# Loading the input X in two halves of 64 partitions from two DMA queues

## The reference

```
x = layer_norm(x, ln_in_g, ln_in_b)
c_act = silu(c)
ada = c_act @ w_ada + b_ada            # shift, scale and gate vectors, 9 of width 1024
h = x * (1 + scale) + shift            # the first of the three modulations
x = layer_norm(ALPHA * x + 0.5 * gate * swiglu(h, ffn1_w_in, ffn1_w_out), ...)
```

## Time and profile before

| | |
|---|---|
| median of 3 runs | 1103.38 us (1103.23 to 1103.72) |
| the profiled execution, its time | 1103.3 us |
| its span, from the first to the last instruction | 1101.5 us |
| granted clock of the matrix engine | 1.00 |
| PE busy | 1094.1 us (99% of the span) |
| DVE, ACT, POOL busy | 520.8, 415.3, 510.8 us |
| data moved | 142.11 MB, mean 129 GB/s |

### The profile page before, as it was taken

The page is one execution under the profiler, slowest core; times in us unless marked ns, Lnnn a source line. Parts: engine busy times, 40 slices in busy tenths (PEclk is TensorE's granted clock), DMA queues, the critical chain, the costliest instruction groups (busy, mean ns, idle before and its releaser), DMA issues.

```text
span 1101.5 us, 15344 instructions
## 1 busy us (share of the span) xinstructions
PE 1094.1 (99%) x5568; PEld 894.5 (81%) x5568; DVE 520.8 (47%) x934; ACT 415.3 (38%) x671; POOL 510.8 (46%) x274
## 2 busy tenths in 40 slices
PE   9999999999999999999999999999999999999998
PEld 6788888888888997875578888898888888888887
DVE  6767755441121269368747677684222223211105
ACT  5552332223222284278623233357222222232223
POOL 1035554444454464357824454646444444445452
PEclk9999999999999999999999999999999999999999
DMA  9555555322333272210136654414433332233322
GB/s 368 208 188 202 179 194 172 105 96 86 92 102 105 74 256 100 87 58 1 49 125 209 218 167 150 150 43 138 150 115 114 114 114 95 90 93 102 105 70 77
DMA packets 53747, 142.11 MB, mean 129 GB/s; under 512 B 5824, under 2 KB 14016, under 8 KB 52416
## 3 DMA queue, kind: packets, MB, share of 16 engines
q1 hardware_dynamic: 52976, 136.40, 37.6%
q10 hardware_dynamic: 720, 5.03, 1.2%
HBM read 139.31 MB, written 2.10 MB: 128 GB/s over the span
## 4 chain that ended last, share of the span: by engine, by line
PE 96%; DMA 1%; DVE 1%; SPq 1%; ACT 0%; issue 0%; POOL 0%; ACTq 0%; DVEq 0%
PE psum L711 30%; PE psum L713 29%; PE psum L712 29%; PE psum L1124 2%; PE psum L1203 2%; PE psum L1175 2%; DMA ada_first<-in_ada 1%; PE psum L1059 1%; PE psum L741 1%; PE psum L1189 0%; PE psum L1095 0%; SPq L518 0%; PE psum L849 0%; ACT tokens L1511 0%; PE psum L1041 0%
## 5 line engine op out<-in xcount | busy, mean ns | idle before, releaser
L600 POOL TENSOR_TENSOR w_lo<-raw,w_hi 128x1024 fp32r<-128x1024 f32 x171 | 422.4, 2475 | 505.3 <-ACT w_hi L1315 505.3
L711 PE MATMUL psum<-h_hi,w_hi 128*128 128x512 f32 (+1 forms) x1006 | 381.3, 379 | 0.2 <-POOL h_lo L654 0.2
L713 PE MATMUL psum<-h_hi,w_lo 128*128 128x512 f32 (+1 forms) x1006 | 378.0, 376 | 0.0
L712 PE MATMUL psum<-h_lo,w_hi 128*128 128x512 f32 (+1 forms) x1006 | 377.9, 376 | 0.0
L1315 ACT ACTIVATE w_hi<-raw 128x1024 fp32r<-128x1024 f32 x178 | 186.4, 1052 | 144.6 <-PE psum L713 94.6
L711 PEld LDWEIGHTS psum<-h_hi,w_hi 128*128 128x128 f32 x1006 | 189.2, 188 | 39.2 <-issue 4.5
L713 PEld LDWEIGHTS psum<-h_hi,w_lo 128*128 128x128 f32 x1006 | 189.3, 188 | 34.7
L712 PEld LDWEIGHTS psum<-h_lo,w_hi 128*128 128x128 f32 x1006 | 189.3, 188 | 33.4
L2054 DVE SCALAR_TENSOR_TENSOR acc<-ada_raw,cact,acc 128x512 f32<-128x512 f32 x98 | 138.5, 1448 | 16.7 <-DMA ada_raw<-in_ada_w 16.6
L711 PE MATMUL psum<-act_hi,w_hi 128*128 128x512 f32 (+1 forms) x396 | 145.3, 367 | 0.0
L713 PE MATMUL psum<-act_hi,w_lo 128*128 128x512 f32 (+1 forms) x396 | 144.7, 365 | 0.0
(11 more groups left out here) (300 smaller groups left out, 1013.1 us busy)
## 6 DMA issues: line engine op xcount, KB each, us to landing
raw<-in_ffn_in SPq DMA_DIRECT2D x81, 512.0 KB, 3.2
ada_raw<-in_ada_w SPq DMA_DIRECT2D x112, 256.0 KB, 3.5
raw<-in_ffn_out SPq DMA_DIRECT2D x32, 448.0 KB, 3.3
raw<-in_mix_w SPq DMA_DIRECT2D x27, 512.0 KB, 3.3
ada_first<-in_ada SPq DMA_DIRECT2D x8, 1024.0 KB, 7.8
raw<-in_ffn_out SPq DMA_DIRECT2D x16, 512.0 KB, 3.5
raw<-in_branch_w SPq DMA_DIRECT2D x8, 512.0 KB, 3.9
raw<-in_mixout_w SPq DMA_DIRECT2D x8, 512.0 KB, 3.4
```

Of the source, the lines that this page charges most:

```text
L600: gp.tensor_tensor(w_lo[:, slot, :], raw[:, slot % 2, :], w_hi[:, slot, :].bitcast(F32), ALU.subtract).then_inc(split_done, 1)
L711: pe.matmul(o_, w[0][:, wslot, ws], xh, start=first, stop=False)
L712: pe.matmul(o_, w[0][:, wslot, ws], xl, start=False, stop=False)
L713: return pe.matmul(o_, w[1][:, wslot, ws], xh, start=False, stop=last)
```

## The change

Each of the five pieces of X is issued as two DMAs of 64 partitions: partitions 0 to 63 by SP as before, partitions 64 to 127 by ACT, before ACT's first table load. Both raise the same semaphore of the piece by 16, so everyone who waits for a piece waits for 32 in place of 16. No other transfer, and no computation, is changed.

```
-                sp.dma_start(X[:, a:z, :], xT[:, a:z, :]).then_inc(x_landed[i], 16)
+                sp.dma_start(X[0:64, a:z, :], xT[0:64, a:z, :]).then_inc(x_landed[i], 16)
...
-                    pe.wait_ge(x_landed[i], 16)
+                    pe.wait_ge(x_landed[i], 32)
...
+            for i, (a, z) in enumerate(X_LOADS):
+                act.dma_start(X[64:P, a:z, :], xT[64:P, a:z, :]).then_inc(x_landed[i], 16)
             act.preload_act_table(ACT.Tanh)
             for m in SQ_ACT:
-                act.wait_ge(x_landed[X_LOAD_OF[m]], 16)
+                act.wait_ge(x_landed[X_LOAD_OF[m]], 32)
                 act.activation(hbuf[:, m, :], X[:, m, :], ACT.Square).then_inc(x_squared_act, 1)
-            act.wait_ge(x_landed[X_LOAD_OF[KT - 1]], 16)
+            act.wait_ge(x_landed[X_LOAD_OF[KT - 1]], 32)
...
-                dve.wait_ge(x_landed[X_LOAD_OF[m]], 16)
+                dve.wait_ge(x_landed[X_LOAD_OF[m]], 32)
```

## The result

| | before | after |
|---|---|---|
| median | 1103.35 us (17 runs, 1103.18 to 1103.88) | 1105.61 us (17 runs, 1105.31 to 1106.1) |
| ratio | | 1.0021, 95% interval 1.0014 to 1.0027 |
| span of the profiled execution | 1101.5 us | 1103.9 us |

The change costs 2.26 us. The forecast was 1103.3 with a range up to 1104.5, so the time lies outside of it. It is about the size that the prediction called the edge of what can be told (2.2 us); with 17 runs each the interval is clear of 1, so the loss is real, though small.

A forecast was written before the change was run, and what follows sets the result against it. PE's gapless matmuls were taken to bound the kernel, so only the head, where loads stand in one line, counts. Terms -0.20 + 0.15 = -0.05 us on 1103.3 made 1103.25, with 0.08 for the median 1103.3; range 1102.6 to 1104.5.

The forecast's parts named there:

- What bounds the kernel: Whole kernel: gapless PE matmuls after the head, so head gains or losses pass to the end one for one.
- The slack of 0.28: Before line 741: PE waits 0.28 us for the third ada_first load, so X could come that much later without harm.
- SP's issues: SP's five X issues, now for 64 partitions: pitch unchanged at about 0.52 us, cost 0.
- ACT's issues: ACT's five new X issues at the start: 2.3 us, at worst 3.7, hidden by ACT's wait for the second piece; cost 0.
- The bytes: X's loading from 3.5 us on: same 2 MB, engines already full at 398 GB/s, so cost 0.
- The first two microseconds: From 1.5 to 3.5 us: a second queue fills idle engine time, between 0 and -0.39 us, taken as -0.20.
- Five more DMAs: Loading of X: completions of five further DMAs cost 0 to 0.30 us, taken as +0.15.
- Half-speed writes: Rival, loading of X: 64-partition transfers reach half the write paths, +5.0 to +5.3 us, 1108.3 to 1108.6; chance 0.05.
- The halves out of step: Rival, head: SP's later loads compete with ACT's remaining X, giving 1103.7 to 1105.0 us, likeliest 1104.1; chance 0.13.
- two queues sharing something: Sign of a wrong prediction: SP's issues lengthen because both queues share descriptor making, pitch well above 0.52 us on both.

The follow-up runs named there:

- The four probes: Kernel before plus 2 MB extra loads ahead of X: partitions 0-63, 32-95, all 128, or both halves from two queues; 1116.91, 1113.34, 1111.21, 1115.26 us.
- the ten full DMAs: Against the kernel before, X loaded in ten DMAs over all 128 partitions; from SP and ACT 1103.72 us, all from SP 1105.22 us.
- the run with quarters: Against the changed kernel, SP loads partitions 32-95 of each piece, ACT 0-31 and 96-127 in two DMAs; 1108.08 us.
- the probe pair: Kernel before plus 2 MB loaded ahead of X, partitions 0-63 by SP and 64-127 by ACT at the same time; 1115.26 us.
- the probe of the middle: Kernel before plus 2 MB loaded by SP ahead of X into partitions 32-95, in four DMAs; 1113.34 us.
- the full one: Kernel before plus 2 MB loaded by SP ahead of X over all 128 partitions, in two DMAs; 1111.21 us.

## Why the prediction was wrong, point by point

**What bounds the kernel** was right. The head is passed on to the end: 1080.75 us from line 741 on, against a stated 1080.9. The slack of 0.28 us played little part, since the third ada_first load was late with X (2.52 us against 2.60), as said for causes that act on the whole line.

**SP's issues, "I take no change; cost 0"** was wrong in its number and right in its cost. An issue of 64 partitions takes longer, not less: a pitch of 3.16 / 5 = 0.63 us in place of 0.52. The loads behind were queued 0.55 us later (colv at 3.94 against 3.39), while the engines were full (share 1.02), which speaks for a cost of nothing; no run measures it alone.

**ACT's issues** ended at 4.19 us, the table load at 5.5, between the two ends given (4.4 and 5.7). ACT's first square waited for its piece until 8.05. Hidden, as stated.

**"The bytes. ... Cost 0"** is the step that failed. It took the rate of 398 GB/s as a property of full engines. It is not: it holds for the loads into all partitions that the rows showed. In the change the same engines, as full, moved 253 GB/s: in 5.5 us 0.80 MB less, which is 2.0 us at 398 GB/s, of the 2.64 us by which X was late. The four probes showed why: what the engines move when full depends on the place of the partitions that they write.

**The first two microseconds**, put at -0.20 between 0 and -0.39, brought nothing: 137 GB/s against 139, at a lower share (0.51 against 0.64). The stretch itself is not fixed: the ten full DMAs moved 122 GB/s in it from two queues and 203 from one, and no layout had any piece of X read earlier than before. Its bound of no gain was right.

**Five more DMAs**, put at +0.15 with a bound of 0.30, is 0.39 us of arrival from two queues with all partitions, with the shorter rows and the second queue in it: somewhat over the bound. From one queue, a case that the term did not speak of, it is 1.83 us.

**The rivals.** Half-speed writes had a chance of 0.05; it was the mechanism. The point from which it was to decide was well placed: over 2.5 us longer, under 270 GB/s; measured were 2.64 us and 253 GB/s, and a loss of 0.21%. Its price of +5.0 to +5.3 us was twice too large, because it let the two halves never overlap: alone, one half does go at 213 GB/s, but the two halves together reach 253 to 309, and the first 2 us, limited otherwise, lost nothing. The halves out of step happened little in the change (by 10 us SP's queue had moved 1.03 MB and ACT's 0.96) and much in the run with quarters. The half-speed case was set low by the argument that with both queues filled each engine has both kinds of rows at hand. That was the error in it: in the probe pair both queues were filled and had about the same share of the engines (46.0% each from 7 to 8 us), and the rate was 262 GB/s there and 309 from 4 to 7 us. Why both kinds of rows at hand do not help more stays open.

## What to carry to other kernels

A transfer should write to all 128 partitions, or at least to a range that reaches all write paths: 64 partitions from 0 went at half the rate (213 of 423 GB/s), 64 from 32 at over nine tenths (388). If a load must be shared between two queues, share it by columns or tiles, not by partitions; here that undid most of the loss, but with the DMA engines already full it won nothing. A DMA share of 1.0 does not say that the rate is what it could be; read GB/s beside it.

## What the runs showed of the hardware

An issue of 64 partitions kept the queue longer than one of 128, whether the 64 began at partition 0, 32 or 64. One line's instructions in the probe of the middle, and in the full one (ns, min/median/max):

```profile
L520 SPq DMA_DIRECT2D X<-in_xT x2: 581/612/642, 0.7 to 1.4; - x2
```

```profile
L520 SPq DMA_DIRECT2D X<-in_xT x1: 411/411/411, 0.7 to 0.7; - x1
```

0.61 us against 0.41, for half the bytes. The same longer issues stand in the kernel with the halves on one queue (0.58 to 0.60 us for either half), so it is not two queues sharing something, as the prediction had offered.

A share near 1.0 with half the rate (213 against 423 GB/s) is how these transfers into half of the partitions look: the engines count as busy although they move less. The share with a low rate does not name the cause by itself: ten small DMAs over all partitions from one queue had a share of 0.99 at 334 GB/s.
